# A state output table made in 32 pieces inside an expert loop

## The chip, the cores and the metric

The kernel runs on one core of a Trainium2 chip. The metric is the time of one execution on the device, in microseconds. Before the change three runs gave 2605.81, 2607.7 and 2612.88 us, a median of 2607.7 us.

The engines that matter are TensorE (PE in the profile), VectorE (DVE), ScalarE (ACT) and GpSimd (POOL); SyncE (SP) only issues DMAs. SP's DMAs are queue q1 in the profile, ScalarE's q10, GpSimd's q0. All share 16 DMA engines.

## The reference

Two blocks on 512 tokens of width 1024, in float32. The first: a retention and pooling mixer, then a routed mixture of 32 experts with 4 per token, then a gated per-layer product ("ple"). The second begins with a state space mixer (s5), followed by feed-forward layers and a convolution mixer. The part of s5 that concerns us:

```python
mag = jnp.exp(lr * dt)
abr = mag * jnp.cos(li * dt)          # one complex number per group and state
abi = mag * jnp.sin(li * dt)
...
_, _, xr, xi = lax.associative_scan(_ssm_combine, (a_r, a_i, bu_re, bu_im), axis=1)
y = (jnp.einsum('ghp,blgp->blgh', c_re.astype(f32), xr)
     - jnp.einsum('ghp,blgp->blgh', c_im.astype(f32), xi))
```

There are 64 groups with 64 complex states and 16 channels each. The kernel takes the sequence in chunks of 8 tokens. What a chunk's incoming state adds to its 8 outputs is the state times a table m_c: for each group, step v of the chunk (8) and channel (16), the entry is `c_re * power_re(v) + c_im * power_im(v)`, with the signs folded into c. The table has 128 partitions (real and imaginary parts of 64 states) by 64 x 8 x 16 = 8192 columns, 4.19 MB. It depends on weights alone.

## The kernel before

It is one program written out by hand: each engine has its own list of instructions, and semaphores order them across engines. The stages are the mixer, the routing, the expert loop, the combine with the ple stage, the s5 mixer, and the remaining linear layers.

**The expert loop.** For each of the 32 experts twelve slots of weights, 1 MB each, are loaded by SP into the tile `ring` (8 of the up projection, 4 of the down projection). A slot is reloaded when TensorE has done with it. For full precision each slot is split in two: ScalarE makes the high part (`slot_hi`, L1065, four buffers), VectorE the rest (`slot_lo`, L1854), and TensorE multiplies both (L2540). The splits are made three slots ahead of their use. Between them VectorE does the activation function (`swiglu`, L1846 to L1848), and the low parts of the hidden activations (`hidden_low`, L1863) and of the tokens (`tokens_low`, L1870). In the function `expert` a counter j of 0 to 11 says behind which split each of these stands: `swiglu` at j == 1 and j == 7, `hidden_low` at 5, `tokens_low` at 9. POOL gathers the next expert's tokens (`next_tile`) once per expert, ScalarE stores each expert's result to `y_dram`.

**Behind the loop.** SP loads the rows of p, the two halves of the ple gate weights (`ple_w_sb[0]` when the last slots are free, `ple_w_sb[1]` when the last `y_dram` store has landed), and later, when the third token tile is combined, `k_dram` into `m_t`; then two rows of `mod_dram` and, in halves, `m_w_dram` into `m_w`. POOL gathers four rows of `y_dram` per token from the 16 tiles `got` (`take`, L829), four gathers of 512 KB for each of the four token tiles, the last four only after a step of the first tile's norm. VectorE's order there is: 6 instructions of the table (`two_powers(0)`, `two_powers(2)`, L1949 to L1951), `add_down_bias` for the four token tiles (L1937, from TensorE's product L2627), `combine_main(0)` (L1956, four instructions), `c_power(4)` (L1941 to L1943), `combine_main(1)` and `(2)`, `c_power(5)`, `ple_add(0)` (L1971, L1972), `combine_main(3)`, `z_rows(0)`, `two_powers(6)`, `ple_add(1)`, then the angles of the recurrence, `ple_add(2)`, the tiles of u (L1981, L1982) and `ple_add(3)`. So the table m_c is made in five calls, two steps v at a time or one, in `ring` columns 0 to 8191, which are slots 0 to 3 of the expert loop.

TensorE's order there is: the bias products (L2627), the transposes of p (L2302), `ple_product` of tiles 0 and 1 (L2652), then for each token tile its transposes (`token_columns`, L2302, behind its combine) and two gate products of 8 steps (`ple_gate`, L2644). ScalarE takes each gate product (L1213). The table is first read in `state_rows`, far behind, when the s5 recurrence has made its states.

Of the kernel before, what the change touches and what calls it, by code (L numbers as in the profile page):

```python
# [15 lines left out]
F32 = mybir.dt.float32  # L16
# [3 lines left out]
ALU = mybir.AluOpType  # L20
# [97 lines left out]
def program(nc, a, out):  # L118
    with ExitStack() as ctx:
# [10 lines left out]
        def sem(name):  # L130
            return ctx.enter_context(nc.semaphore(name))
# [80 lines left out]
        s5_tb = work[:, 5120:6144].rearrange("p (g h) -> p g h", g=G)  # L212
        s5_tb2 = work[:, 4096:6144].rearrange("p (g v h) -> p g v h", g=G, v=2)
# [42 lines left out]
        mod_bc = [work[:, 8192 + 1024 * v:9216 + 1024 * v].rearrange("p (g h) -> p g h", g=G) for v in range(2)]  # L256
        theta, mag_gp = sm[:, 16:16 + GP], sm[:, 48:48 + GP]
# [72 lines left out]
        m_w_dram = nc.dram_tensor("m_w_dram", [P, G * 2 * NS], F32).ap()  # L330
        k_dram = nc.dram_tensor("k_dram", [GC, G, 2 * CH, GC], F32).ap()
# [125 lines left out]
        s_gelu_ready = sem("gelu_ready")  # L457

# [91 lines left out]
        def _(sp):  # L550
            def load(dst, src, done):
                sp.dma_start(dst, src).then_inc(done, 16)
# [106 lines left out]
            sp.wait_ge(s_norm_in, 112)  # L659
            load(p_rows, p_by_chunk, s_ple_in)  # L660
# [5 lines left out]
            load(ple_w_sb[1], ple_gate_v[:, :, 512:1024], s_ple_in)  # L666
            sp.wait_ge(s_got_used, 2)
# [67 lines left out]
        def _(pool):  # L735
# [68 lines left out]
            def next_tile(tile):  # L804
                pool.wait_ge(s_xs_in, tile * 16 + (HN_STORED + 16))
                pool.wait_ge(s_xt_ready, 2 * tile + 2)
                gather(tile + 1)
# [7 lines left out]

            with pool.Fori(0, E) as e:
                next_tile(e)
            pool.wait_ge(s_route_ok, 2)
# [604 lines left out]
        def _(dve):  # L1423
# [448 lines left out]

            def expert(e, follows=True):

                for j in range(12):
                    if j == 9 and not follows:
                        tokens_low(e + 1)
                        swiglu(e, 1)
                    low_ahead(e, j)
                    if j == 1:  # L1880
                        swiglu(e - 1, 1)
                    if j == 5:
                        hidden_low(e - 1)
                    if j == 7:
                        swiglu(e, 0)
                    if j == 9 and follows:
                        tokens_low(e + 1)
                    if j == 9 and not follows:
                        hidden_low(e)
# [15 lines left out]
            split_low(1, 2)  # L1905
            expert(1)
            per = 2 * 2
# [11 lines left out]
            with dve.If(extra > 0):  # L1919
                main_step, step = step, Steps(dve, s_dve_more)  # L1920
                with dve.Fori(0, extra) as n:
                    step.n, step.off = 0, n * per
                    for j in range(SPLIT):
                        if j == 8:
                            swiglu(n + E, 0)
                            swiglu(n + E, 1)
                            hidden_low(n + E)
                            tokens_low(n + E + 1)
                        dve.wait_ge(s_slot_hi, n * SPLIT + (E * SPLIT + j + 1))
                        tt(slot_lo[:, j], slot[j], whole(slot_hi[j % HI_BUFS]), ALU.subtract).then_inc(s_slot_lo, 1)  # L1930
                step = main_step
# [6 lines left out]

            def c_power(v):
                ar, ai = [power[:, r, v, :].unsqueeze(2).broadcast_to([P, G, GC]) for r in range(2)]  # L1940
                step(tt(m_c[:, :, v, :], s5c[0], ar, ALU.mult))  # L1941
                step(tt(s5_tb, s5c[1], ai, ALU.mult))
                step(tt(m_c[:, :, v, :], m_c[:, :, v, :], s5_tb, ALU.add))  # L1943

            def two_powers(v):
                both = [P, G, 2, GC]
                ar, ai = [power[:, r, v:v + 2, :].rearrange("p v g -> p g v").unsqueeze(3).broadcast_to(both) for r in range(2)]
                c_re, c_im = [x.unsqueeze(2).broadcast_to(both) for x in s5c]
                step(tt(m_c[:, :, v:v + 2, :], c_re, ar, ALU.mult))  # L1949
                step(tt(s5_tb2, c_im, ai, ALU.mult))  # L1950
                step(tt(m_c[:, :, v:v + 2, :], m_c[:, :, v:v + 2, :], s5_tb2, ALU.add))  # L1951
# [46 lines left out]
            dve.wait_ge(s_ct_sb, 2)  # L1998
            dve.wait_ge(s_power_ok, 2)
            two_powers(0)  # L2000
            two_powers(2)
# [11 lines left out]
            c_power(4)  # L2013
            combine_main(1)
            combine_main(2)
            c_power(5)
# [4 lines left out]
            two_powers(6)  # L2021
# [266 lines left out]
        def _(pe):  # L2288
# [474 lines left out]
            def state_rows(k):  # L2763
                pe.wait_ge(s_x_state, k // 2 + 1)
                for j in range(4 * k, 4 * k + 4):
                    for two in range(2):
                        last = mm(row_bank(k, j, two), x_s[:, 2 * j + two, :], m_c[:, 2 * j + two].rearrange("p s h -> p (s h)"), start=False, stop=(j == 4 * k + 3))
                last.then_inc(s_yo_ps, 1)
# [193 lines left out]
```

## Time and profile before

| | us |
|---|---|
| median of three runs | 2607.7 |
| span of the profiled execution | 2610.7 |
| TensorE busy | 2542.8 (97%) |
| VectorE busy | 1946.6 (75%) |
| ScalarE busy | 1354.3 (52%) |
| GpSimd busy | 212.5 (8%) |
| first to last store of an expert's result | 352.8 to 1424.7 |

The span is the profiled execution's own time from its first to its last instruction; the page gives no other time for it. It lies 3.0 us over the median and inside the range of the runs.

The page cuts the span in 40 slices of 65 us. The expert loop fills slices 5 to 20 and part of 21. In 5 to 20 TensorE and VectorE both show 9 (90% or more busy) and the DMA engines move 380 to 411 GB/s. From slice 21 on the DMA queues move less.

A timeline row gives start and length in us, engine, line, operation, output tile and inputs, how many instructions are merged, and in brackets the idle time before them and what ended it. A row of a group gives busy us, mean ns of one instruction, and the idle time before. A row of a stretch gives its length, then busy us and count of PE, PEld, DVE, ACT, POOL, then the granted TensorE clock as a share of full speed, the DMA share and GB/s. A share of the DMA engines a little over 100% is a full queue.

### The profile page before, as it was taken

The page shows a single profiled execution, that of the slowest core. Times are in us where ns is not written, and L with a number is a line of the kernel's source. Part 1 is how long each engine was busy: PE and PEld are TensorE (multiplying, and loading weights), DVE is VectorE, ACT ScalarE, POOL GpSimd, SP SyncE. Part 2 cuts the span into 40 slices and gives each one's busy share as a digit, 9 for nine tenths or more (in the row PEclk, how much of TensorE's full clock was granted, in tenths as well). Part 3 has the DMA queues.
Part 4 walks back from the last instruction along what each step waited for, and adds up shares of the span by engine and source line. Part 5 has one row for each costly group of instructions (what it writes and reads, how often), then busy time and mean ns, then how long its engine had stood idle before and what let it go on. Part 6 is the DMA issues. An engine that isn't in the chain of part 4 may idle for free.

```text
span 2610.7 us, 34375 instructions
## 1 busy us (share of the span) xinstructions
PE 2542.8 (97%) x12258; PEld 2082.5 (80%) x12258; DVE 1946.6 (75%) x1843; ACT 1354.3 (52%) x1361; POOL 212.5 (8%) x323
## 2 busy tenths in 40 slices
PE   9998999999999999999998979999999999999998
PEld 7777788888888888888886468888888888888886
DVE  7878999999999999999999877788632544433422
ACT  5233777777777777777775354322222222222322
POOL 2150100000000000000000311111000000000000
PEclk9998999999999999999999999999999999999999
DMA  9535899999999999999995936377443531233332
GB/s 330 201 104 182 318 399 411 395 385 386 386 381 389 387 380 390 385 385 383 390 381 216 202 117 202 118 245 241 145 109 98 154 97 40 65 96 96 107 90 77
DMA packets 351758, 643.92 MB, mean 247 GB/s; under 512 B 27152, under 2 KB 220560, under 8 KB 350928
## 3 DMA queue, kind: packets, MB, share of 16 engines
q1 hardware_dynamic: 327600, 540.83, 60.5%
q0 software_dynamic: 17872, 78.13, 8.4%
q10 hardware_dynamic: 6224, 24.12, 2.3%
q8 instruction: 40, 0.66, 0.1%
q14 instruction: 22, 0.18, 0.0%
HBM read 616.87 MB, written 26.16 MB: 246 GB/s over the span
## 4 chain that ended last, share of the span: by engine, by line
PE 71%; issue 15%; DVE 10%; DMA 2%; ACT 1%; POOL 1%; ACTq 0%; POOLq 0%; DVEq 0%; SPq 0%
PE bank L2540 39%; PE bank L2804 8%; PE bank L2805 8%; PE bank L2812 8%; PE bank L2528 1%; PE bank L2523 1%; PE bank L2516 1%; PE bank L2334 1%; DMA ring<-in_w_in 1%; DVE slot_lo L1854 1%; DVE rows L1956 1%; PE bank L2363 1%; PE bank L2365 1%; PE bank L2364 1%; DVE cb L1507 1%
## 5 line engine op out<-in xcount | busy, mean ns | idle before, releaser
L1854 DVE TENSOR_TENSOR slot_lo<-ring,slot_hi 128x2048 fp32r<-128x2048 f32 x384 | 864.3, 2286 | 68.2 <-ACT slot_hi L1065 67.1
L1065 ACT ACTIVATE slot_hi<-ring 128x2048 fp32r<-128x2048 f32 x384 | 736.3, 1920 | 252.2 <-PE bank L2540 224.9
L2540 PE MATMUL bank<-slot_hi,xs_hi 128*128 128x512 f32 x1024 | 315.5, 389 | 1.1 <-issue 1.1
L2540 PE MATMUL bank<-slot_hi,xs_lo 128*128 128x512 f32 x1024 | 315.3, 389 | 0.0
L2804 PE MATMUL bank<-h_hi,fin_hi 128*128 128x512 f32 x704 | 274.2, 390 | 0.7 <-DVE fin_lo L2121 0.7
L2540 PE MATMUL bank<-slot_lo,xs_hi 128*128 128x512 f32 x1024 | 274.3, 390 | 0.5 <-DVE slot_lo L1854 0.5
L2805 PE MATMUL bank<-h_hi,fin_lo 128*128 128x512 f32 x704 | 273.9, 389 | 0.0
L2540 PEld LDWEIGHTS bank<-slot_hi,xs_hi 128*128 128x128 f32 x1024 | 192.2, 188 | 41.6 <-issue 1.5
L2540 PEld LDWEIGHTS bank<-slot_lo,xs_hi 128*128 128x128 f32 x1024 | 192.1, 188 | 41.0 <-DVE slot_lo L1854 1.3
L2540 PEld LDWEIGHTS bank<-slot_hi,xs_lo 128*128 128x128 f32 x1024 | 192.2, 188 | 40.1
L2121 DVE TENSOR_TENSOR fin_lo<-rows,fin_hi 128x1024 fp32r<-128x1024 f32 x88 | 103.7, 1222 | 127.5 <-ACT fin_hi L1324 127.3
L1324 ACT ACTIVATE fin_hi<-rows 128x1024 fp32r<-128x1024 f32 x88 | 88.2, 1052 | 212.3 <-DMA rows<-in_w_ffn_in 212.3
L2812 PE MATMUL bank<-h_lo,fin_hi 128*128 128x512 f32 x704 | 166.7, 389 | 0.0
L2540 PE MATMUL bank<-slot_hi,act_hi 128*128 128x512 f32 x512 | 161.4, 396 | 2.7 <-DVE act_lo L1863 2.7
L2540 PE MATMUL bank<-slot_hi,act_lo 128*128 128x512 f32 x512 | 158.9, 392 | 0.0
L2804 PEld LDWEIGHTS bank<-h_hi,fin_hi 128*128 128x128 f32 x704 | 132.1, 188 | 28.9 <-issue 1.5
L2812 PEld LDWEIGHTS bank<-h_lo,fin_hi 128*128 128x128 f32 x704 | 132.2, 188 | 27.4
L2805 PEld LDWEIGHTS bank<-h_hi,fin_lo 128*128 128x128 f32 x704 | 132.2, 188 | 27.4
L2804 PE MATMUL bank<-f_hi,fout_hi 128*128 128x512 f32 x352 | 137.7, 391 | 0.0
L2540 PE MATMUL bank<-slot_lo,act_hi 128*128 128x512 f32 x512 | 137.2, 390 | 0.0
L2805 PE MATMUL bank<-f_hi,fout_lo 128*128 128x512 f32 x352 | 137.0, 389 | 0.0
L1368 ACT ACTIVATE ring<-bank 128x512 f32<-128x512 f32 x60 | 35.8, 597 | 184.5 <-PE bank L2812 184.5
(476 smaller groups left out, 4003.3 us busy)
## 6 DMA issues: line engine op xcount, KB each, us to landing
ring<-in_expert_w_gate_up SPq DMA_DIRECT2D x256, 1024.0 KB, 7.2
ring<-in_expert_w_down SPq DMA_DIRECT2D x128, 1024.0 KB, 6.7
rows<-in_w_ffn_in SPq DMA_DIRECT2D x88, 512.0 KB, 5.0
work<-in_w_ada POOLq DMA_DIRECT2D x64, 384.0 KB, 4.4
y_dram<-cb ACTq DMA_DIRECT2D x32, 512.0 KB, 7.3
ring<-in_w_ada POOLq DMA_DIRECT2D x36, 384.0 KB, 5.1
work<-in_w_ffn_out SPq DMA_DIRECT2D x8, 1408.0 KB, 7.0
rows<-in_w_ffn_out SPq DMA_DIRECT2D x8, 1408.0 KB, 7.0
```

Of the source, the lines that this page charges most:

```text
L1065: act.activation(hi_of(e, j), slot[q], ACT.Copy).then_inc(s_slot_hi, 1)
L1324: act.activation(split[n][0][b][:, v], raw[:, v], ACT.Copy).then_inc(s_w_hi, 1)
L1368: act.activation(sig_sb[b], ps[3 * b + bank][:], func).then_inc(s_lin_sig, 1)
L1507: return stt(acc, w, cact[:, k:k + 1], acc, ALU.mult, ALU.add)
L1854: tt(slot_lo[:, q], slot[q], whole(hi_of(e, j)), ALU.subtract).then_inc(s_slot_lo, 1)
L1956: ins = stt(rows[:, i, :], got[n], weights[:, n:n + 1], rows[:, i, :], ALU.mult, ALU.add)
L2121: tt(split[n][1][at][:, v], buf[at][:, v], whole(split[n][0][b][:, v]), ALU.subtract).then_inc(s_w_lo, 1)
L2334: last = mm(proj_bank(i), x[:, k, P * i:P * (i + 1)], w[:, k, :], start=(k == 0 and part == 0), stop=(k == KD - 1 and part == 2))
L2540: last = mm(ps[banks + n], x[:, k, :], (lo if lower else hi)[:, k, 512 * n:512 * (n + 1)], start=(begins and lower == 0 and k == 0 and x i ...
L2804: mm(ps[3 * b + v][:], w_hi[b][:, v, k, :], x_hi[:, k, :], start=(k == 0), stop=False)
L2805: mm(ps[3 * b + v][:], lo[:, v, k, :], x_hi[:, k, :], start=False, stop=False)
L2812: last = mm(ps[3 * b + v][:], w_hi[b][:, v, k, :], x_lo[:, k, :], start=False, stop=(k == depth[n] - 1))
```

## The change

The table is no longer made behind the loop. Inside the loop, behind the split at j == 4 of each expert, VectorE makes the 1/32 of it that belongs to 2 of the 64 groups, in a buffer of 256 columns (`mc_part`) with a second one for the other product (`mc_tmp`). POOL stores each piece to the new tensor `m_c_dram`, 128 rows of 1 KB at a pitch of 32 KB, and VectorE waits before each piece for the store of the one before. Piece 0 is made ahead of `expert(1)`, pieces 1 to 31 in the experts of that number. SP loads the whole table, 128 rows of 32 KB, behind the second half of the gate weights. TensorE waits for it in `state_rows`. SP also waits for the 32 stores before it loads the rows of p, which go where the pieces were.

```diff
+        MC_COLS = G * CH * GC // E
+        mc_part, mc_tmp = work[:, 8192:8192 + MC_COLS], work[:, 8192 + MC_COLS:8192 + 2 * MC_COLS]
...
             sp.wait_ge(s_norm_in, 112)
+            sp.wait_ge(s_mc_stored, 16 * E)
             load(p_rows, p_by_chunk, s_ple_in)
...
             load(ple_w_sb[1], ple_gate_v[:, :, 512:1024], s_ple_in)
+            load(m_c[:].rearrange("p g s h -> p (g s h)"), m_c_dram, s_mc_in)
             sp.wait_ge(s_got_used, 2)
...
+            def store_part(e):
+                pool.wait_ge(s_mc_ready, e + 1)
+                pool.dma_start(m_c_dram[:, bass.ds(MC_COLS * e, MC_COLS)], mc_part).then_inc(s_mc_stored, 16)
+
             with pool.Fori(0, E) as e:
                 next_tile(e)
+                store_part(e)
...
+            gl = G // E
+
+            def state_part(e):
+
+                at = bass.ds(gl * e, gl)
+                of_part = [P, gl, CH, GC]
+                part, tmp = [v.rearrange("p (g v h) -> p g v h", g=gl, v=CH) for v in (mc_part, mc_tmp)]
+                ar, ai = [power[:, r, :, at].rearrange("p v g -> p g v").unsqueeze(3).broadcast_to(of_part) for r in range(2)]
+                c_re, c_im = [v[:, at, :].unsqueeze(2).broadcast_to(of_part) for v in s5c]
+                if not (isinstance(e, int) and e == 0):
+                    dve.wait_ge(s_mc_stored, 16 * e)
+                step.go(tt(part, c_re, ar, ALU.mult))
+                step(tt(tmp, c_im, ai, ALU.mult))
+                tt(part, part, tmp, ALU.add).then_inc(s_mc_ready, 1)
...
                     low_ahead(e, j)
+                    if j == 4:
+                        state_part(e)
                     if j == 1:
                         swiglu(e - 1, 1)
...
+            dve.wait_ge(s_gates_ps, 1)
+            dve.wait_ge(s_ct_sb, 2)
+            dve.wait_ge(s_power_ok, 2)
+            state_part(0)
             expert(1)
...
-            def c_power(v):
-                ar, ai = [power[:, r, v, :].unsqueeze(2).broadcast_to([P, G, GC]) for r in range(2)]
-                step(tt(m_c[:, :, v, :], s5c[0], ar, ALU.mult))
-                step(tt(s5_tb, s5c[1], ai, ALU.mult))
-                step(tt(m_c[:, :, v, :], m_c[:, :, v, :], s5_tb, ALU.add))
-
-            def two_powers(v):
...
-            two_powers(0)
-            two_powers(2)
             for i in range(NT):
                 add_down_bias(i)
...
             combine_main(0)
-            c_power(4)
             combine_main(1)
             combine_main(2)
-            c_power(5)
             ple_add(0)
             combine_main(3)
             dve.wait_ge(s_norm_in, 128)
             z_rows(0)
-            two_powers(6)
             ple_add(1)
...
             def state_rows(k):
                 pe.wait_ge(s_x_state, k // 2 + 1)
+                if k == 0:
+                    pe.wait_ge(s_mc_in, 16)
```

## Rows read from the trace of the kernel before

**Rows 1.** Page part 4: share of the span on the chain that ended last, by engine.
```profile
PE 71%; issue 15%; DVE 10%; DMA 2%; ACT 1%; POOL 1%; ACTq 0%; POOLq 0%; DVEq 0%; SPq 0%
```

**Rows 2.** Groups by form, 700 to 1390 us: busy us, mean ns, idle before and releaser.
```profile
L1854 DVE TENSOR_TENSOR slot_lo<-ring,slot_hi 128x2048 fp32r<-128x2048 f32 x235 | 529.2, 2286 | 43.7 <-ACT slot_hi L1065 43.0
```

**Rows 3.** Busy time by stretch: PE, PEld, DVE, ACT, POOL, PEclk, DMA share, GB/s.
```profile
734.50:769.00 34.50, 34.50 (x162) 28.73 (x161) 32.18 (x23) 26.55 (x23) 1.87 (x3) 1.00 1.01 385
...
1442.00:1444.00 2.00, 2.00 (x3) 0.67 (x2) 1.61 (x2) 2.00 (x4) 1.39 (x3) 0.50 1.02 412
1444.00:1446.00 2.00, 2.00 (x5) 0.91 (x4) 1.96 (x2) 0.05 (x1) 1.47 (x2) 0.82 1.02 410
1448.60:1515.30 66.70, 65.77 (x177) 30.55 (x175) 57.68 (x55) 27.22 (x41) 18.41 (x25) 1.00 1.05 170
```

**Rows 4.** DVE timeline, 900 to 945 us: start, us, line, idle before and releaser.
```profile
921.77 6.69 DVE L1854 TENSOR_TENSOR slot_lo<-ring,slot_hi 128x2048 fp32r<-128x2048 f32 x3
929.73 2.29 DVE L1854 TENSOR_TENSOR slot_lo<-ring,slot_hi 128x2048 fp32r<-128x2048 f32 x1 [1.27 <-ACT slot_hi L1065]
```

**Rows 5.** PE timeline, same stretch.
```profile
938.47 1.08 PE L2540 MATMUL bank<-slot_lo,act_hi 128*128 128x512 f32 x4
```

**Rows 6.** POOL timeline, same stretch.
```profile
901.60 0.70 POOL L796 COPY smi<-smi 128x1 int32 x1 [33.28 <-PE bank L2516]
...
936.96 0.71 POOL L796 COPY smi<-smi 128x1 int32 x1 [33.27 <-PE bank L2516]
```

**Rows 7.** DVE groups by form, 300 to 1850 us.
```profile
L1949 DVE TENSOR_TENSOR ring<-work,cb 128x2048 f32<-128x2048 f32 x3 | 6.9, 2288 | 0.0
...
L1941 DVE TENSOR_TENSOR ring<-work,cb 128x1024 f32<-128x1024 f32 x2 | 2.4, 1219 | 0.0
```

**Rows 8.** PE timeline, 1400 to 1620 us.
```profile
1425.12 4.76 PE L2627 MATMUL bank<-work 32*128 32x512 f32 x16 [1.56 <-issue]
...
1438.79 10.04 PE L2652 MATMUL bank<-work,ca 128*128 128x512 f32 x16 [0.78 <-ACT ca L903]
1448.67 1.04 PE L2302 MATMUL bank<-const,rows 128*128 128x128 f32 x8
```

**Rows 9.** DVE timeline, 1395 to 1620 us.
```profile
1432.51 4.62 DVE L1937 TENSOR_TENSOR rows<-rows,bank 128x1024 f32<-128x1024 f32 x4
1442.35 5.25 DVE L1956 SCALAR_TENSOR_TENSOR rows<-ring,sm,rows 128x1024 f32<-128x1024 f32 x4 [5.23 <-DMA ring<-y_dram,smi]
...
1511.27 1.28 DVE L1981 SCALAR_TENSOR_TENSOR cb<-nat,sm,work 128x1024 f32<-128x1024 f32 x1 [7.18 <-POOLq L861]
...
1516.75 0.69 DVE L1971 TENSOR_TENSOR nat<-nat,bank 128x512 f32<-128x512 f32 x1 [0.23 <-DVE cb L1982]
```

**Rows 10.** SP queue timeline, 1330 to 1620 us: the DMA issues.
```profile
1429.52 0.37 SPq L552 DMA_DIRECT2D ring<-in_ple_gate_w  x1
...
1461.79 28.29 SPq L552 DMA_DIRECT2D ring<-k_dram  x8
...
1505.44 10.11 SPq L552 DMA_DIRECT2D ring<-m_w_dram  x2
```

**Rows 11.** DMA queues, 1433 to 1436 us: packets, MB, share of 16 engines.
```profile
q1 hardware_dynamic: 590, 1.21, 105.3%
```

**Rows 12.** DMA queues, 1436 to 1439 us.
```profile
q0 software_dynamic: 267, 1.03, 86.1%
q1 hardware_dynamic: 115, 0.20, 18.4%
```

**Rows 13.** DMA queues, 61 to 62 us, two loads in flight on two queues.
```profile
q0 software_dynamic: 59, 0.29, 74.7%
q1 hardware_dynamic: 57, 0.12, 31.8%
```

**Rows 14.** DMA packets by size, 1505 to 1523 us.
```profile
DMA packets 504, 4.95 MB, mean 275 GB/s; under 512 B 64, under 2 KB 64, under 8 KB 248
```

**Rows 15.** ACT timeline, 1395 to 1620 us.
```profile
1515.24 0.69 ACT L1213 ACTIVATE nat<-bank,sm 128x512 f32<-128x512 f32 x1 [1.13 <-PE bank L2644]
```

More of the change, by code:

```diff
@@ L211, in program @@
         k_turn = work[:, 0:2048].rearrange("p (q t) -> p q t", q=G // 4)
-        s5_tb = work[:, 5120:6144].rearrange("p (g h) -> p g h", g=G)
-        s5_tb2 = work[:, 4096:6144].rearrange("p (g v h) -> p g v h", g=G, v=2)
         k_sb = cb[:, 0:1024].rearrange("p (g h) -> p g h", g=G)
@@ L330, in program @@
         m_w_dram = nc.dram_tensor("m_w_dram", [P, G * 2 * NS], F32).ap()
+        m_c_dram = nc.dram_tensor("m_c_dram", [P, G * CH * GC], F32).ap()
         k_dram = nc.dram_tensor("k_dram", [GC, G, 2 * CH, GC], F32).ap()
@@ L457, in program @@
         s_gelu_ready = sem("gelu_ready")
+        s_mc_ready = sem("mc_ready")
+        s_mc_stored = sem("mc_stored")
+        s_mc_in = sem("mc_in")
         ctx.enter_context(nc.allow_non_contiguous_dma(reason="columns of weights"))
@@ L1905, in _ @@
             split_low(1, 2)
+            dve.wait_ge(s_gates_ps, 1)
+            dve.wait_ge(s_ct_sb, 2)
+            dve.wait_ge(s_power_ok, 2)
+            state_part(0)
             expert(1)
-            per = 2 * 2
+            per = 2 * 2 + 2
             n0 = step.n
@@ L1921, in _ @@
                 with dve.Fori(0, extra) as n:
-                    step.n, step.off = 0, n * per
+                    step.n, step.off = 0, n * 4
                     for j in range(SPLIT):
@@ L1937, in add_down_bias @@
                 tt(rows[:, i, :], rows[:, i, :], pairs[i][:], ALU.add).then_inc(s_prep_dve, 1)
-            def c_power(v):
-                ar, ai = [power[:, r, v, :].unsqueeze(2).broadcast_to([P, G, GC]) for r in range(2)]
-                step(tt(m_c[:, :, v, :], s5c[0], ar, ALU.mult))
-                step(tt(s5_tb, s5c[1], ai, ALU.mult))
-                step(tt(m_c[:, :, v, :], m_c[:, :, v, :], s5_tb, ALU.add))
-            def two_powers(v):
[L1946 to L1951, printed above, removed]
             def combine(i, weights, done):
@@ L1996, in reduce_turns @@
                 reduce_angle(rot_s[:, at], rot_s[:, at], rot_c[:, at])
-            dve.wait_ge(s_ct_sb, 2)
-            dve.wait_ge(s_power_ok, 2)
-            two_powers(0)
-            two_powers(2)
             for i in range(NT):
```

## The prediction

> **What bounds the kernel now.** I read the chain that ended last first. TensorE carries 71% of it and VectorE 10% [rows 1], so an edit of VectorE work is worth only what it moves TensorE. In the expert loop the groups show VectorE nearly full, and the only thing it waits for is ScalarE's high half of a weight slot: 43.7 us in the 690 us of the stretch [rows 2]. One expert takes 936.96 - 901.60 = 35.36 us, by POOL's copy that comes round once per expert [rows 6]; 690/35.36 is 19.5 experts, so VectorE is idle 2.24 us per expert. TensorE is busy in every microsecond of the 34.5 us stretch, at full clock [rows 3]. So TensorE sets the loop's pace and VectorE has 2.24 us to spare.
>
> Behind the loop the picture looks different at first: VectorE is busy from 1418 us on, and three groups of the removed code stand on the chain. But the stretch 1448.60 to 1515.30 has TensorE busy 65.77 of 66.70 us [rows 3]: it begins with the transposes of the first combined token tile at 1448.67 [rows 8] and ends with the last gate product, which ScalarE takes at 1515.24 [rows 15]. Inside it VectorE works for TensorE's products and is ahead of what TensorE wants. What decides is when that block starts and when it is picked up. It starts when the products of the p projection are done (1438.79 + 10.04 = 1448.8, at half clock [rows 8, 3]) and when the first combine is done (1442.35 + 5.25 = 1447.6 [rows 9]). And that combine waited 5.23 us for the gather of y_dram [rows 9].
>
> **The change part by part.**
>
> *The 32 pieces in the loop.* Each is three tensor_tensor of 256 columns. The trace has the same operations at 2048 and 1024 columns, 2288 and 1219 ns [rows 7]: 1.044 ns per column and 150 ns besides, so about 417 ns for 256, and three with their two hand-overs about 1.3 us. Bounds: 3 x 0.15 = 0.45 us if the columns were free, and 3 x 0.69 = 2.1 us by the 512-column row [rows 9]; I take 1.3 us, since the form is the same and only the length is extrapolated. Both ends lie under the 2.24 us. The place is good too: the piece stands behind the split that the code calls j == 4, and there VectorE now ends at 921.77 + 6.69 = 928.46 and sits idle 1.27 us until 929.73 [rows 4]. The next split, first of the down weights, is wanted by TensorE at 938.47 [rows 5] and ends at 932.02, so a late piece has 6.4 us before TensorE would see it. Behind VectorE's added wait on the store of the previous piece (131 KB, a whole expert earlier) stand that split and all that follow; the store has 35 us for a transfer whose like here take single microseconds. Without that cover the loop would pay 31 x 1.3 = 40 us. Cost: 0, range 0 to 1.
>
> *POOL's store.* It adds one wait and one DMA issue per expert, between two gathers. POOL idles 33.28 us of each 35.36 [rows 6], and the piece is ready in the first half of an expert, before the next gather's wait ends. Bytes: 0.13 MB on top of 385 GB/s x 35.36 us = 13.6 MB, one per cent; the queues moved 410 to 412 GB/s where they were full [rows 3], so 389 still fits. No instruction of the loop waits for a load (ScalarE's slots wait for TensorE to free buffers). Cost 0; at worst, if 385 were the ceiling, 0.34 us per expert of lag, 11 us at the end. A slot is loaded when it is freed, twelve slot times before its next use, and ScalarE splits it four ahead: 8 x 2.7 = 22 us, less 7 to land, 15 us of cover. I keep 1 us as upper end.
>
> *Piece 0 and piece 31.* Piece 0 puts 1.3 us in front of the first experts' splits; TensorE's margin there is of the same size as in the loop except for one transpose. 0, at most 0.3 us. The last piece is ready at j == 4 of the last expert, near 1395, and SP's added wait on its store is reached only after the expert loads, at 1409: nothing queued behind it waits longer.
>
> *What goes behind the loop.* Nine instructions of 2048 columns (9 x 2.29 = 20.6 us) and six of 1024 (6 x 1.22 = 7.3 us [rows 7]): 27.9 us of VectorE. The six in front of the bias adds let those start when TensorE's bias products come (from 1426.3, by four of sixteen in 1425.12 + 4.76 [rows 8]) instead of at 1432.51 [rows 9]. They then end at about 1431.2, not 1437.1. The p transposes and products, which wait for them, come 6 us earlier and end near 1442.9 even at half clock. Then combine 0 is what TensorE waits for: 1447.6 instead of 1448.67, a gain of 1.1 us. The rest of the 27.9 us lies beside the 66.7 us block and buys nothing in it. At its end a little more: the last ple_add starts at 1516.75 because two u tiles stand before it (they started at 1511.27 [rows 9]), while its gate is ready at 1515.93 [rows 15]; those u tiles come earlier, so 0.8 us go. All VectorE relief together: 1.1 + 0.8 = 1.9 us.
>
> *The load of m_c.* This is the term that decides. 4.19 MB are issued on SP's queue right behind the second gate weight load (1429.52 [rows 10]), 0.6 us before POOL issues the first gather. In the trace the 16 engines are full there: SP's queue alone takes 105% from 1433 to 1436 [rows 11]; its last 0.20 MB are gone half a microsecond into the next stretch, at 1436.5, and then the gathers have the engines to themselves (86% [rows 12]). Four gathers are 2.10 MB: 2.10/0.412 [rows 3] = 5.1 us, to 1441.6, and combine 0 starts 0.7 us later.
>
> Now m_c's rows stand in SP's queue when the gate weights are through. How do two queues share? Where two loads with different row lengths are in flight, each gets the same number of packets, not of bytes: 59 against 57, with 0.29 against 0.12 MB [rows 13]. The long rows win. m_w's rows of 16 KB go as single packets (256 of the 504 packets are over 8 KB, and they carry 2 x 2.1 MB [rows 14]); m_c's rows are 32 KB against the gather's 4 KB. With one for one the gather gets 1/9 of the time, or 1/5 if a packet ends at 16 KB; either way m_c is through before the first four gathers are, and combine 0 sees both amounts: (4.19 + 2.10)/0.412 = 15.3 us in place of 5.1. Combine 0 starts at 1452.5 and ends at 1457.8. That is +9.1 us on the start of TensorE's block (1457.8 - 1448.67). Lower bound of the delay: 0, if the gathers went first (then the -1.1 above); upper bound the 10.2 us of m_c's bytes.
>
> The Trainium skill (DMA: Bandwidth & Descriptors, SWDGE vs HWDGE vs iDMA) calls a packet, the engine's switching boundary, preferably at most 4096 B. By that m_c's rows would be cut into the gather's size, the shares would be even, and the sum would be that of rival 1. The trace speaks against it for SP's queue, with its packets of 16 KB [rows 14].
>
> *The clock.* TensorE now has nothing from 1442.9 to 1457.8. In the trace it works from 1438.79 and its granted clock is still 0.50 (1.2 of 2.4 GHz) in 1442 to 1444 and 0.82 in 1444 to 1446 [rows 8, 3]: some 6 us at half clock after a shorter pause. Now those 6 us fall on the first gate products instead of on the p products: 3 us of their work are lost. Bounds: 0 (the clock is up in time), 4.5 us (9 us at half). I take 3.
>
> *Who else is moved.* Combine 1 and 2 get their data at 1457.5 and 1462.6 and run behind combine 0, so combine 2 ends near 1468.2; SP starts the slow k_dram loads on it, 1461.79 now [rows 10], so 6.5 us later, and with them the m_w loads (1505.44) by at most 12, which the first chunk sums, themselves 11 later, still meet. The added wait of TensorE for m_c (landed by 1450) comes a hundred us later: nothing.
>
> *Sum.* 9.1 + 3.0 - 0.8 = +11.3 us, everything in the loop 0. Against the profile's span of 2610.7 that is 2622.0. That span is 3.0 us over the median of 2607.7, so for the median: 2619.0.
>
> **The rivals.**
>
> 1. Even shares. Long rows are cut, gather and m_c take half each: combine 0 has its data after 10.2 us, +5.1. Block start 1452.7 - 1448.67 = +4.0, clock +3, hand-over -0.8: +6.2, 2613.9. For it: two queues do share; against: [rows 13, 14].
>
> 2. The gathers are not delayed at all (the other side). Place: the DMA engines at 1436; mechanism: POOL's packets, once they are there, are served first and m_c gets what is left. Then only -1.1 - 0.8 = -1.9 us stay: 2605.8. It decides once combine 0 is delayed by less than some 2 us. For it: after 1436.5 the gathers do take all the engines [rows 12], but then SP's queue is empty; against it: while SP's queue is full it holds 105% of them, with the first gather already issued [rows 11], and [rows 13].
>
> 3. VectorE bounds the tail. If the chain of waits is taken at its word, the removed groups on it (1.22 x 6 and 2.29 x 3) are worth 14.2 us, 2593.5, and all 27.9 us would give 2579.8. Against it: TensorE's 65.77 of 66.70 us.
>
> 4. The loop turns to VectorE's pace. From 2.24 us per piece on (say that the addresses, which now depend on the expert, cost as much as the arithmetic: 2.6 us) each expert pays the excess: 0.36 x 31 = 11 us more, 2630. Against it: the bounds 0.45 to 2.1.
>
> **How the numbers follow.** Forecast 0.62, rival 1 0.15, rival 2 0.10, rival 3 0.05, rival 4 0.08. The forecast's own range is 2615 to 2623 (clock 0 to 4.5, loop 0 to 2). The range for 8 in 10 goes down to rival 2 and a little past the forecast's upper end: 2605 to 2626. A change under 0.3% (7.8 us) can't be told from none. Faster by more, under 2599.9: rival 3 and a remainder, 0.06. Within: rivals 1 and 2 and a little of the forecast, 0.27. Slower, over 2615.5: 0.67.
>
> **What would show it.** Right: in the changed trace combine 0 starts near 1452.5 plus what the loop shifts, waiting for the gather, and the queue's rows show SP's queue with most of the bytes from 1436 to 1447; the first gate product runs at a granted clock of 0.5; an expert still takes 35.36 us and VectorE's idle time per expert falls from 2.2 to about 0.9 us. Wrong: the gather lands near 1442 (rival 2), the block 1448 to 1515 shrinks (rival 3), or an expert takes over 35.5 us (rival 4).

## The result, and the profile after

The changed kernel takes 2619.2 us (median of 6 runs, 2616.02 to 2623.9), the kernel before 2607.43 us beside it (6 runs, 2604.89 to 2612.88). The ratio is 1.0042, 95% interval 1.0028 to 1.0055: slower by 0.4%. Forecast were 2619.0 us and a range of 2605 to 2626. The profiled execution took 2623.9 us, with a span of 2622.3, against the span of 2610.7 before: +11.6 us, where +11.3 were forecast. In every execution on record the time is 1.5 to 1.8 us over the span. By that the profiled execution before took about 2612.4 us (an estimate), so both profiled executions lie about 5 us over their medians, and the spans compare like with like.

**The chain.** First the line that answers to [rows 1], part 4 of the page after.

```profile
PE 74%; issue 15%; DVE 8%; DMA 2%; ACT 1%; ACTq 0%; SPq 0%; POOLq 0%; POOL 0%; DVEq 0%
```

VectorE's share of the chain fell from 10% to 8%, so the work was taken off the chain as meant, and the kernel is still slower. A share of the chain says who is on it, not what its removal gives.

**The loop.** Groups of VectorE by form, 700 to 1390 us (answers to [rows 2]; columns as there):

```profile
L1865 DVE TENSOR_TENSOR slot_lo<-ring,slot_hi 128x2048 fp32r<-128x2048 f32 x235 | 528.8, 2284 | 21.2 <-ACT slot_hi L1076 21.1
L1897 DVE TENSOR_TENSOR work<-work 128x256 f32<-128x256 f32 x20 | 8.5, 425 | 0.7
L1895 DVE TENSOR_TENSOR work<-work,cb 128x256 f32 x19 | 7.9, 416 | 0.0
L1896 DVE TENSOR_TENSOR work<-cb 128x256 f32 x19 | 7.9, 415 | 0.0
```

The pieces cost 415 to 425 ns an instruction, and the idle time in front of `slot_lo` fell from 43.7 to 21.2 us. The 24.3 us of these three rows stand almost wholly in time that was idle. What is left of it is 21.2/19.5 = 1.09 us per expert, where I had forecast about 0.9. POOL's timeline, 895 to 945 us, gives the pace (answers to [rows 6]):

```profile
902.16 0.71 POOL L802 COPY smi<-smi 128x1 int32 x1 [6.16 <-PE bank L2527]
...
930.78 0.59 POOL L824 DMA_DIRECT2D m_c_dram<-work  x1 [26.50 <-DVE work L1897]
937.52 0.71 POOL L802 COPY smi<-smi 128x1 int32 x1 [6.15 <-PE bank L2527]
```

937.52 - 902.16 = 35.36 us per expert, as before. POOL's store stands in the middle of its idle time.

**Behind the loop.** SP's queue, 1395 to 1620 us (answers to [rows 10]):

```profile
1430.02 0.37 SPq L556 DMA_DIRECT2D ring<-in_ple_gate_w  x1
1430.43 0.58 SPq L556 DMA_DIRECT2D ring<-m_c_dram  x1
...
1468.49 31.91 SPq L556 DMA_DIRECT2D ring<-k_dram  x8
...
1517.60 10.62 SPq L556 DMA_DIRECT2D ring<-m_w_dram  x2
```

VectorE, 1400 to 1530 us (answers to [rows 9]):

```profile
1427.06 4.61 DVE L1969 TENSOR_TENSOR rows<-rows,bank 128x1024 f32<-128x1024 f32 x4 [7.88 <-PE bank L2638]
1452.83 10.42 DVE L1974 SCALAR_TENSOR_TENSOR rows<-ring,sm,rows 128x1024 f32<-128x1024 f32 x8 [21.17 <-DMA ring<-y_dram,smi]
...
1527.52 0.69 DVE L1989 TENSOR_TENSOR nat<-nat,bank 128x512 f32<-128x512 f32 x1 [0.23 <-DVE cb L2000]
```

TensorE, 1425 to 1530 us (answers to [rows 8]):

```profile
1434.53 8.80 PE L2663 MATMUL bank<-work,ca 128*128 128x512 f32 x16 [2.84 <-ACT ca L914]
1458.18 1.94 PE L2313 MATMUL bank<-const,rows 128*128 128x128 f32 x8 [14.85 <-issue]
1460.90 9.40 PE L2655 MATMUL bank<-ring,ca 128*128 128x512 f32 x16 [0.78 <-ACT ca L914]
...
1520.84 7.03 PE L2655 MATMUL bank<-ring,ca 128*128 128x512 f32 x16
```

The first combine waits 21.17 us for the gather where it waited 5.23, and starts at 1452.83 instead of 1442.35. TensorE has nothing for 14.85 us ahead of the first transposes. Its sixteen first gate products then take 9.40 us, where those of the last tile take 7.03. The stretches (columns as in [rows 3]) say why:

```profile
1450.00:1452.00 2.00, 0.00 (x0) 0.00 (x0) 0.00 (x0) 0.00 (x0) 0.00 (x0) 0.50 0.99 395
...
1458.00:1460.00 2.00, 1.82 (x8) 1.57 (x8) 1.97 (x3) 1.75 (x3) 0.56 (x2) 0.50 1.03 410
1462.00:1464.00 2.00, 2.00 (x4) 0.90 (x3) 2.00 (x2) 0.71 (x1) 1.70 (x2) 0.50 0.42 68
1464.00:1466.00 2.00, 2.00 (x4) 0.80 (x3) 1.93 (x3) 0.44 (x2) 1.39 (x3) 0.62 0.84 274
1466.00:1468.00 2.00, 2.00 (x7) 0.81 (x6) 1.96 (x2) 0.00 (x0) 1.85 (x3) 1.00 0.88 320
```

While every compute engine is idle the DMA engines are full, at 395 GB/s, and the granted clock (first of the last three columns) is at 0.50 until past 1464. Who has the DMA engines? The queues (packets, MB, share of 16 engines) at 1436 to 1439 us, when SP's queue still holds gate weights:

```profile
q0 software_dynamic: 208, 0.79, 66.4%
q1 hardware_dynamic: 214, 0.46, 39.9%
```

and at 1442 to 1445 us, when it holds the table:

```profile
q1 hardware_dynamic: 36, 1.18, 91.4%
q0 software_dynamic: 36, 0.09, 7.3%
```

About as many packets from each queue in both, very unequal bytes in the second: 1.18 MB in 36 packets is a whole 32 KB row in each. The gather gets 0.09 of 1.27 MB; 15 of the 72 packets are under 512 B, so not all of its 36 are 4 KB rows.

### The profile page after: what moved, and what is told of

Its sections match the earlier page's. It is cut to its first block, busy times and chain, and to the rows that moved or that the text cites. A ratio compares the mean times of both kernels' runs of the same rounds, so it can differ in the third digit from the quotient of the medians.

```text
span 2622.3 us, 34699 instructions
## 1 busy us (share of the span) xinstructions
PE 2543.8 (97%) x12258; PEld 2082.6 (79%) x12258; DVE 1953.0 (74%) x1924; ACT 1353.9 (52%) x1361; POOL 228.7 (9%) x355
## 4 chain that ended last, share of the span: by engine, by line
PE 74%; issue 15%; DVE 8%; DMA 2%; ACT 1%; ACTq 0%; SPq 0%; POOLq 0%; POOL 0%; DVEq 0%
PE bank L2551 39%; PE bank L2817 8%; PE bank L2825 8%; PE bank L2818 8%; PE bank L2655 2%; PE bank L2539 1%; PE bank L2534 1%; PE bank L2527 1%; DMA ring<-in_w_in 1%; PE bank L2345 1%; DVE slot_lo L1865 1%; PE bank L2313 1%; PE bank L2663 1%; PE bank L2374 1%; PE bank L2375 1%
```

## The experiments

The kernel before was run beside each group of four: 2609.75, 2610.01 and 2609.37 us (29, 23 and 28 runs). Ratios are to it, with 95% intervals; 0.001 is 2.6 us. The single runs of one kernel lie up to 16 us apart, so where a few us matter I also measure inside the traces, from one event: S is the issue of the second gate weight load, which comes when the last `y_dram` store has landed, and so does the gather. C is the start of the first combine, T TensorE's first transposes of a combined tile. The block is from T to the end of the last gate product. Each line is one trace. (e8_gate_early is not in the table: there the second gate weights are loaded before that store has landed, so its S is another event.)

| kernel | S to C | S to T | block | ratio |
|---|---|---|---|---|
| before | 12.83 | 19.15 | 66.53 | 1 |
| changed | 22.81 | 28.16 | 69.69 | 1.0042 |
| e1_late | 13.08 | 18.43 | 69.40 | 1.0001 |
| e2_4k | 16.30 | 21.65 | 68.85 | 1.0021 |
| e3_nopieces_late | 12.67 | 18.02 | 66.86 | 1.0003 |
| e4_nopieces_early | 22.37 | 27.72 | 69.67 | 1.0047 |
| e5_pieces_only | 15.12 | 22.08 | 66.53 | 0.9999 |
| e6_warm | 22.56 | 27.86 | 68.84 | 1.0037 |
| e7_triple | 23.29 | 28.64 | 70.45 | 1.0179 |
| e9_warm36 | 23.84 | 29.14 | 69.47 | 1.0049 |
| e10_late_warm | 13.05 | 18.35 | 70.14 | 0.9994 |
| e11_2k | 14.51 | 19.86 | 68.89 | 1.0019 |
| e12_8k | 19.02 | 24.37 | 69.94 | 1.0020 |

### e1_late: the same load, later

```diff
             load(ple_w_sb[1], ple_gate_v[:, :, 512:1024], s_ple_in)
-            load(m_c[:].rearrange("p g s h -> p (g s h)"), m_c_dram, s_mc_in)
...
                      m_w_dram.rearrange("p (g m) -> p g m", g=G)[:, GP * half:GP * (half + 1), :], s_t_in)
+            load(m_c[:].rearrange("p g s h -> p (g s h)"), m_c_dram, s_mc_in)
```

> The table's load is issued behind the last m_w load on SP's queue, some 90 us later; all else as in the changed kernel. If the load in front of the gathers costs the time (my account: 9 us later start of the gate block and 3 us of half clock), combine 0 starts near 1442 to 1444 us again and the time falls to the kernel before or 2 us under it: 2605.5, and I allow 2603 to 2608. If the pieces in the loop, their stores or the new waits cost it, the time stays near 2619. If the late load itself delays the m_w loads or the state rows, it stands between, near 2612.

Measured: 2609.82 us, ratio 1.0001 (0.9992 to 1.0009), level with before, and above the 2603 to 2608 that I had allowed. One line moved takes back all that the change cost. The small gain that VectorE's relief should leave is not to be seen; more on that below.

### e2_4k: the same place, short rows

```diff
-            load(m_c[:].rearrange("p g s h -> p (g s h)"), m_c_dram, s_mc_in)
+            for n in range(8):
+                load(ring[:, 1024 * n:1024 * (n + 1)], m_c_dram[:, 1024 * n:1024 * (n + 1)], s_mc_in)
```

> The table is loaded at the same place of SP's queue, but as eight loads of 1024 columns, so that its rows are 4 KB like the gather's. Packet-for-packet sharing: the gather gets half the engines in place of a ninth, its first 2.1 MB take 10.2 us in place of 15.3, combine 0 starts some 5 us earlier than in the changed kernel, near 1447.5, and the time is near 2614. If SP's queue is simply served before POOL's, or if what counts is the sum of the bytes, combine 0 stays at 1452.5 and the time at 2619. The rows of all packets would then show no gather packets from 1437 to 1447.

Measured: 2614.76 us, ratio 1.0021 (1.0011 to 1.003): about half of the cost is gone with no byte fewer. The first combine starts 6.5 us earlier from S, where I had expected 5; e11_2k and e12_8k below show why. The queues of this kernel, 1439 to 1442 us:

```profile
q1 hardware_dynamic: 172, 0.64, 53.5%
q0 software_dynamic: 170, 0.60, 49.6%
```

Again as many packets from each, and now as many bytes.

### e3_nopieces_late and e4_nopieces_early: no table at all

Both leave out the computation of the table: no pieces, no stores, nothing behind the loop, and the 4.19 MB are read from `m_w_dram` instead. They differ only in where the load stands.

```diff
-                store_part(e)
...
-                    if j == 4:
-                        state_part(e)
...
-            load(m_c[:].rearrange("p g s h -> p (g s h)"), m_c_dram, s_mc_in)
+            load(m_c[:].rearrange("p g s h -> p (g s h)"), m_w_dram, s_mc_in)
```

> No pieces and no stores in the loop; the table is left out altogether and the same 4.19 MB are read from m_w's table in DRAM in its place, late, behind the last m_w load, so the output is of another table. Against the kernel before this is VectorE's relief behind the loop alone. My account: -1.9 us, 2605.5. If VectorE bounds the stage behind the loop, 2593 (the removed groups on the chain) or 2580 (all of them). Against e1_late it shows what pieces and stores cost: 0 to 1 us by my account.

> As e3_nopieces_late (the table left out, no pieces, no stores), but the 4.19 MB are read where the changed kernel reads its table, behind the second gate weight load. If the place of the load is the whole cost, this is as slow as the changed kernel, 2618 to 2619, and 12 to 13 us over e3_nopieces_late. If the loop pays a part, it is faster than the changed kernel by that part.

Measured: late 2609.52 us, 1.0003 (0.9994 to 1.0012); early 2620.95 us, 1.0047 (1.0034 to 1.0059). The place of the load alone is worth 11.4 us, as much as the whole change (0.0044 against 0.0042). And a kernel that never makes the table is no faster than one that makes it behind the loop. I had expected 1.9 us of relief for it; its interval, -1.6 to +3.1 us, leaves that out by a little. So VectorE's relief as forecast was missed here, not only hidden in the noise; see the relief below.

### e5_pieces_only: the loop's half of the change

The kernel before, with the pieces and stores added in the loop. The table is still made behind the loop, and `m_c_dram` is not read.

```diff
             with pool.Fori(0, E) as e:
                 next_tile(e)
+                store_part(e)
...
                     low_ahead(e, j)
+                    if j == 4:
+                        state_part(e)
```

> The kernel before with the 32 pieces and their stores added inside the loop; the table is also still made behind the loop as before, and m_c_dram is never loaded. So only what the loop half of the change costs is added. My theory (pieces and POOL stores lie in idle time of VectorE and POOL): 0 to +1 us on the runs of the kernel before, 2609.8 to 2611, and the last y_dram store issues within 1 us of 1424.7. Rival (the loop half costs by itself, through VectorE's pace or POOL's queue, and e1_late only hides it with the relief behind the loop): +2 to +11 us, 2612 to 2621.

Measured: 2609.39 us, ratio 0.9999 (0.999 to 1.0009). The loop's half costs nothing. (Its last `y_dram` store issued at 1421.33; that event lies between 1418 and 1427 in the profiles of all kernels but e7_triple, so the 1 us that I had asked of it was too sharp a mark. From S to T it has 22.08 us where the kernel before has 19.15: its last store landed 2.64 us after its issue instead of 4.80, which puts S earlier, but T was set by VectorE, see the relief below.)

### e7_triple: where the loop's cover ends

```diff
+                for _ in range(2):
+                    step.go(tt(part, c_re, ar, ALU.mult))
+                    step(tt(tmp, c_im, ai, ALU.mult))
+                    step(tt(part, part, tmp, ALU.add))
                 step.go(tt(part, c_re, ar, ALU.mult))
                 step(tt(tmp, c_im, ai, ALU.mult))
```

> The changed kernel with the three operations of each piece done three times over. A piece then costs VectorE 3 x 1.15 = 3.45 us against 2.24 us that it has idle per expert. If the idle time is all there is to hide in (rival 4's threshold): 1.2 us over, times 31 experts = 37 us on 2619.2, about 2656, and ScalarE's part of the idle time is 0 in the loop. If VectorE's real slack is larger, because it idles for other engines' sake and TensorE has buffers in hand: 2619 to 2630. If pieces already cost something in the changed loop: over 2680.

Measured: 2657.44 us, ratio 1.0179 (1.0163 to 1.0195), 38.2 us over the changed kernel's 2619.2. Its POOL timeline:

```profile
888.75 0.72 POOL L802 COPY smi<-smi 128x1 int32 x1 [3.67 <-PE bank L2531]
925.30 0.72 POOL L802 COPY smi<-smi 128x1 int32 x1 [3.67 <-PE bank L2531]
```

and VectorE's groups, 700 to 1390 us:

```profile
L1865 DVE TENSOR_TENSOR slot_lo<-ring,slot_hi 128x2048 fp32r<-128x2048 f32 x228 | 509.7, 2284 | 0.0
```

An expert takes 36.55 us, 1.19 more than 35.36, and VectorE no longer waits for ScalarE: 0.0 where it was 43.7 [rows 2]. 31 x 1.19 = 36.9 us. The forecast of 1.2 us is nearly met, but its 3.45 us for a piece were too small. VectorE's timeline:

```profile
916.66 0.42 DVE L1896 TENSOR_TENSOR work<-work,cb 128x256 f32 x1
...
920.30 2.29 DVE L1865 TENSOR_TENSOR slot_lo<-ring,slot_hi 128x2048 fp32r<-128x2048 f32 x1
```

From the first of the nine operations to the next split it takes 920.30 - 916.66 = 3.64 us, and 3.64 - 2.24 = 1.40 against the 1.19 found. So the 2.24 us per expert are VectorE's whole slack to some 0.2 us. This is rival 4, with its threshold in the right place; the change itself stays under it.

### e6_warm and e9_warm36: TensorE kept busy through its wait

The changed kernel with products that nobody reads (24 in e6_warm, 36 in e9_warm36):

```diff
             pe.wait_ge(s_prep_dve, 6)
+            for _ in range(24):
+                mm(ps[0][:, 0:256], ones, const[:, 0:256], start=True, stop=True)
             token_columns(0)
```

> The changed kernel with 24 extra TensorE products of 256 columns into bank 0, which nobody reads, between TensorE's wait for the first combine's bookkeeping and the transposes of the first token tile, where it now has nothing for 14.9 us. My theory (3 us of the cost is the half clock of the first gate products): the transposes take 1.04 us and the gate products 7.1 us instead of 1.94 and 9.4, and the time is 3 us under the changed kernel's 2619.2: about 2616. Rival (the clock comes back too late anyway, or the extra products are run before the wait and leave a pause behind them): 2619, or up to 2621 if they run into the first transposes.

Measured: 2618.61 us, ratio 1.0037 (1.0023 to 1.005). The products ended at 1446.6 and left 5.89 us before the transposes; the gate products took 8.53 us. So the fill was too short, and I made it longer.

> The changed kernel with 36 extra TensorE products of 256 columns in the same place, in place of the 24 of e6_warm, which lasted 10.5 us and left a pause of 5.9 us in which the clock fell again. 36 last 15.8 us and so reach to the end of the first combine. Theory (the half clock of the first gate products costs some 3 us): transposes of the first token tile 1.04 us, gate products 7.1 us, block from the first transposes to the last gate product 66.7 us in place of 69.7, and 2616 on the runs (ratio to before 1.003). Rival (the block is bound elsewhere and the clock costs nothing): 2619, ratio 1.0042.

Measured: 2622.38 us, ratio 1.0049 (1.0032 to 1.0066): nothing gained. TensorE of e9_warm36:

```profile
1442.89 15.70 PE L2681 MATMUL bank<-const 128*128 128x256 f32 x72
1460.92 1.50 PE L2313 MATMUL bank<-const,rows 128*128 128x128 f32 x8 [2.32 <-DVE rows L1974]
1463.20 9.63 PE L2655 MATMUL bank<-ring,ca 128*128 128x512 f32 x16 [0.78 <-ACT ca L914]
```

and its stretches:

```profile
1456.00:1458.00 2.00, 2.00 (x11) 1.75 (x10) 1.96 (x2) 0.00 (x0) 0.00 (x0) 1.00 1.02 408
1458.00:1460.00 2.00, 0.60 (x3) 0.19 (x1) 1.93 (x3) 0.00 (x0) 0.00 (x0) 1.00 1.03 412
1460.00:1462.00 2.00, 1.08 (x7) 1.08 (x8) 2.00 (x2) 1.10 (x3) 0.00 (x0) 0.87 1.03 410
1462.00:1464.00 2.00, 1.22 (x3) 0.52 (x3) 1.93 (x3) 1.06 (x3) 1.62 (x2) 0.50 0.87 344
```

15.7 us of products at full clock, then a pause of 2.32 us, and the clock is at 0.50 when the gate products begin. Both experiments failed to take the half clock away, so the price of it is read from the traces only, not shown by taking it out.

### e10_late_warm: the best that the experiments pointed to

e1_late with five such products in TensorE's wait (`range(5)` in place of `range(24)`).

> e1_late with 5 extra products of 256 columns in TensorE's wait for the first combine (2.1 us there). In e1_late the clock fell to 0.5 behind that wait and the first gate products took 9.12 us in place of 7.1, and it ended level with the kernel before. Theory (the relief of VectorE is worth 2 to 3 us and the half clock ate it): block shorter by 3 us, 2607, ratio to before 0.999. Rival (so short a fill doesn't hold the clock, or what comes later absorbs it): 2609.8, ratio 1.000.

Measured: 2609.48 us, ratio 0.9994 (0.9983 to 1.0005). No gain that can be told from none. In its profile the gather came later than the fill reached, 4.52 us of pause were left, and the block took 70.14 us, the first products at half clock again. No kernel that I ran beats the kernel before.

### e8_gate_early: the other transfer ahead of the gather

```diff
             sp.wait_ge(s_ple_in, 32)
-            sp.wait_ge(s_y_stored, extra * 16 + 16 * (E + 1))
             load(ple_w_sb[1], ple_gate_v[:, :, 512:1024], s_ple_in)
```

> e1_late (table made in the loop and loaded behind m_w) with the second half of the gate weights loaded without the wait for the last y_dram store. Its 2.1 MB then no longer stand ahead of the first gathers. Theory (after the load of m_c has been put late, the transfers ahead of the gathers are still what the first combine waits for): combine 0 starts 2 to 4 us earlier behind the last y_dram store, TensorE's block with it, less what the p products need: 2606 to 2608. Rival (TensorE's own products, not the gather, set the start now; or the earlier 2.1 MB delay the last y_dram store by as much): 2609.8, no change.

Measured: 2612.47 us, ratio 1.0006 (0.9998 to 1.0015), no gain and rather a loss. Its last `y_dram` store issued at 1423.75 and had landed at 1431.60, when POOL goes on: 7.85 us, where the other kernels need 2.6 to 5.2 to S. From there to C it took 10.56 us instead of 13.1. What the gather won, the store in front of it lost: the rival's case.

### e11_2k and e12_8k: two more row lengths

As e2_4k, with 16 loads of 512 columns (2 KB rows) and 4 of 2048 (8 KB rows).

> The changed kernel with the table loaded as 16 loads of 512 columns in the same place: rows of 2 KB against the gather's 4 KB. Theory (one packet for one): the gather gets 2/3 of the engines, its 2.10 MB take 7.6 us, 2.5 us more than alone and 2.6 less than with 4 KB rows; with e2_4k's 2614.8 that makes 2612, ratio 1.001. Rival (what made e2_4k cheaper was the number of loads, or the queues share by bytes): as e2_4k, 2614.8, ratio 1.002.

> The same with 4 loads of 2048 columns: rows of 8 KB. Theory (one packet for one): the gather gets 1/3, so its first 2.10 MB and the table's 4.19 MB are through together, after 15.3 us, as with 32 KB rows: the whole cost is back already, 2619, ratio 1.004. Rival (the cost grows smoothly with the row from 4 to 32 KB): half way, near 2617.

Measured: 2 KB 2614.94 us, 1.0019 (1.0007 to 1.003); 8 KB 2614.96 us, 1.0020 (1.0007 to 1.0033). Both expectations missed. The queues, 1439 to 1442 us, of e11_2k:

```profile
q0 software_dynamic: 223, 0.83, 69.5%
q1 hardware_dynamic: 221, 0.39, 34.9%
```

and of e12_8k:

```profile
q1 hardware_dynamic: 115, 0.81, 65.2%
q0 software_dynamic: 119, 0.42, 35.2%
```

The shares are those of one packet for one, 2:1 and 1:2. What I had left out is that the gather starts while SP's queue still holds gate weights in 2 KB packets, and gets 0.79 MB through before the table's turn (the rows of 1436 to 1439 above). 2.10 - 0.79 = 1.31 MB are left. Alone they take 1.31/0.412 = 3.2 us; at 2/3, 1/2 and 1/3 of the engines 4.8, 6.4 and 9.5 us; at 1/9 the table is through first, and both take (1.31 + 4.19)/0.412 = 13.3. So the cost should be 1.6, 3.2, 6.3 and 10.1 us. From S to C the traces have +1.4, +3.2, +6.0 and +9.7 over the 13.07 us of e1_late and e10_late_warm. The 0.79 MB were taken from the changed kernel's rows after the runs, so this is an account of them and no forecast. Single traces spread: e3_nopieces_late, late too, has 12.67, and the other kernels with 32 KB rows lie between 22.37 and 23.84, +9.3 to +10.8.

With that, 8 KB rows bring some 60% of the delay (6.0 of 9.7), not all of it. Of the time, the intervals of 8 KB, 4 KB and 32 KB overlap and don't settle it. With 2 KB rows the start of the block is nearly right, but time is lost behind it. SP's queue, the queues at 1463 to 1466 us, and one row of VectorE of e11_2k:

```profile
1429.48 21.65 SPq L556 DMA_DIRECT2D ring<-m_c_dram  x16
...
1465.00 35.76 SPq L556 DMA_DIRECT2D ring<-k_dram  x8
```

```profile
q1 hardware_dynamic: 220, 0.39, 34.4%
q0 software_dynamic: 215, 0.80, 67.7%
```

```profile
1516.95 1.28 DVE L2000 SCALAR_TENSOR_TENSOR cb<-nat,sm,work 128x1024 f32<-128x1024 f32 x1 [12.14 <-DMA work<-mod_dram]
```

The issues last 21.65 us (8 loads: 5.99, 4 loads: 2.02, 1 load: 0.58). The load of `mod_dram`, far behind in the same queue, comes late, and the first u tile waits for it. From the end of the block to the third transpose of the next stage it takes 12.41 us, in the changed kernel 8.10: 4.3 us lost, more than the 1.8 won against 4 KB. (e2_4k waits 9.04 us at the same place and has 9.32 us.) That the number of the loads does it is not shown: all sixteen were issued by 1451.13, 14 us before `k_dram`'s. What the rows show is the other side of the share. With a third of the engines the table is still in the queue at 1466, while the whole 4.19 MB of the changed kernel are through by 1451, and the loads of `k_dram`, issued from 1465.00, stand behind it; their issues last 35.76 us where all other kernels have 28 to 33. How much of the loss is the number of loads and how much the longer transfer is not separated.

## Why the prediction was right, step by step

**The view of the bound held.** TensorE's block sets the end, not VectorE's busy tail. The strongest proof is e3_nopieces_late: 27.9 us of VectorE gone from behind the loop, 1.0003. Rival 3 is out.

**Pieces and stores: 0 forecast, 0 found.** e5_pieces_only has 0.9999; the pieces took 3 x 0.42 us; e7_triple shows the cliff at 2.24 us.

**The load: the right mechanism and the right size.** Forecast: first combine at 1452.5, found 1452.83. In its parts, on the start of the block: forecast +9.1, found 28.16 - 19.15 = +9.01 from S to T. S itself is 0.50 later, by chance: the last store was issued 2.05 us later and landed 1.55 us sooner after its issue. One reading in it was wrong and cost nothing. I had SP's gate weights gone at 1436.5 and the table's turn from then on. In the changed kernel they were still in the queue at 1436 to 1439 and shared the engines with the gather, which moved more bytes than SP's queue there (0.79 against 0.46 MB), where I had forecast most for SP's. The sum of the bytes ahead of the first combine is the same either way, so the 15.3 us stood; for shorter rows it matters, as e11_2k and e12_8k showed. e2_4k, e11_2k, e12_8k and e1_late show by size and by place that it is the sharing of the DMA engines and not, say, SP's wait. Rival 1 (even shares) is what e2_4k does when it is forced, with +3.2 us on the first combine where the rival had +5.1, since the gather has part of its data before the table's turn. Rival 2 (the gather goes first) no row shows. The Trainium skill (DMA: Bandwidth & Descriptors, Queues, rings and completion order) has each engine go round the queues packet by packet, with typically 9 to 17 descriptors drained as one packet. The traces agree on the turns, 36 packets against 36. Another section (SWDGE vs HWDGE vs iDMA) has a packet at 4096 B or less by preference, in its table on the path of GpSimd's DMAs. Of SP's queue the rows show something else: a whole row of 32 KB is counted as one packet.

**The clock: +3.0 forecast, 69.69 - 66.53 = +3.16 found** in the length of the block: 1.94 - 1.04 = 0.90 in the first transposes, 9.40 - 7.10 = 2.30 in the first gate products. That it is the clock rests on the granted clock beside the products' times (9.40 against 7.10 us); the attempts to remove it did not succeed. My account of it was incomplete in one point: I tied it to the long wait. In the profiles, a block that followed TensorE's products without a pause ran at full clock (before, e3_nopieces_late, e5_pieces_only: 66.53 to 66.86 us), and each with a pause of 2.09 us or more ahead of it began at half clock (68.8 to 70.5). It is not so everywhere: e1_late had 2.69 us of pause before the last down products of the loop and stayed at 1.00, the changed kernel had the same pause there and fell to 0.50. And it fell elsewhere without any pause, as the next part shows.

**The relief of VectorE: 1.9 us forecast, not found in the time.** The hand-over at the end of the block is there: 9.36 us to the third transpose became 8.1 (forecast -0.8, found -1.26; e5_pieces_only, which has the old order behind the loop, has 8.78, so about half a microsecond of it is the spread of single traces). So is the earlier start: 18.02 to 18.43 us from S to T in e3_nopieces_late, e10_late_warm and e1_late in place of 19.15, -0.7 to -1.1 (forecast -1.1). How much it is depends on how fast the last store lands. Where it took 4.7 to 4.8 us, T comes 23.95 us after the store's issue before, 23.05 in e10_late_warm. Where it took about 2.6 us, T comes 24.72 us after it in e5_pieces_only, because TensorE waits 4.81 us for the bias adds that stand behind the six table instructions, but 21.09 and 20.66 in e1_late and e3_nopieces_late, which have none there.

In e1_late and e10_late_warm the block starts behind a pause and takes 2.9 and 3.6 us more, which takes the relief back in these two traces. The time of e1_late alone (-2.1 to +2.3 us) would still hold 1.9. But e3_nopieces_late has no such pause: its block is 66.86 us at full clock, and from S to the third transpose its trace is 2.05 us shorter than before's. Its time still shows no gain, and its interval leaves 1.9 out. So the half clock at the block is not the whole account. Its trace lost most of the 2.05 us later, in a stage that the change doesn't touch. The same eight products some 520 us behind the third transpose, from TensorE's timeline of the kernel before (2036 to 2056 us):

```profile
2045.99 1.97 PE L2719 MATMUL bank<-const 128*128 128x256 f32 x8
```

and of e3_nopieces_late (2026 to 2046 us):

```profile
2036.20 3.66 PE L2725 MATMUL bank<-const 128*128 128x256 f32 x8
```

and two stretches of e3_nopieces_late (columns as in [rows 3]):

```profile
2034.00:2036.00 2.00, 2.00 (x20) 2.00 (x19) 0.57 (x1) 0.63 (x1) 0.00 (x0) 1.00 0.50 137
2036.00:2038.00 2.00, 2.00 (x8) 1.66 (x8) 0.16 (x1) 0.00 (x0) 1.02 (x1) 0.56 1.17 323
```

The granted clock fell though TensorE had been busy throughout. e1_late has the same fall (0.52 in 2037 to 2039), the kernel before and the changed one have 1.00 there. Whether it comes with the relief or by chance stays open, and with it where the 1.9 us went.

**The sum** of the parts found: 0.50 + 9.01 + 3.16 - 1.26 = +11.4 of the span's +11.6 us. The relief at the start of the block is part of the 9.01, as it was of the forecast's 9.1. The median's forecast of 2619.0 against 2619.2 owes something to luck: single runs of the changed kernel spread over 8 us.

## What to carry to other kernels

- Before a load is put in front of a transfer that somebody waits for, compare the row lengths, not only the bytes. Here two queues shared packet for packet, and a 32 KB row against 4 KB took nine tenths of the engines; behind the urgent transfer, the same load was free.
- Work moved into another engine's idle time is free up to that idle time per turn and costs every turn beyond it; 43.7 us over 19.5 experts told the limit to some 0.2 us.
- Relief of an engine beside the bound buys only what it moves the bound, and here a shorter job ahead of TensorE's block made a pause in two of three traces, behind which it ran at half clock; in none of the three kernels did it show in the time.

## What the runs showed of the hardware

- SP's queue moves a row of 32 KB as one packet, and where both queues were full it and GpSimd's had about as many packets each at every row length tried (2, 4, 8, 32 KB): 221 and 223, 172 and 170, 115 and 119, 36 and 36 in 3 us.
- A fill of 15.7 us at full clock did not carry the clock over a pause of 2.32 us. In e3_nopieces_late the granted clock fell to 0.56 with TensorE busy 2.00 of 2.00 us in the stretch before.
- A smaller share lasts longer: with 2 KB rows SP's queue got 34 to 37% of the engines and still had the table at 1466, and the issue of its 16 loads took 21.65 us; the 4.19 MB by themselves would need 4.19/0.412 = 10.2 us (an estimate from the full queues' rate).
- Profiles of kernels with the same code up to there have the last `y_dram` store at 1418.7 (e1_late) and 1423.6 (e10_late_warm). Some of it is half clock in the last down products (0.63 and 0.52 in 1410 to 1412 and 1412 to 1414 in the second, 1.00 throughout in the first); what decides it stays open.
